# Order of the bank reads in the first pair of a second-matrix pass, and of the last pass's squares

## What is computed

```python
h = rmsnorm(x, norm_ffn[l])
x = x + jnp.square(jax.nn.relu(h @ w_ff1[l])) @ w_ff2[l]      # w_ff1 1024 x 4096, w_ff2 4096 x 1024
return rmsnorm(x, final_norm)                                  # first_block
...
u = rmsnorm_2(x, ln_g[layer])                                  # second_block, layer 0
proj = u @ w_in
```

## Time and profile before

| | |
|---|---|
| median of three runs | 1632.52 us (1631.73 to 1632.7) |
| the profiled execution, its own time | 1632.63 us |
| its span | 1630.9 us, granted clock 0.999 |
| busy share of the span | PE 98%, PEld 83%, DVE 61%, ACT 54%, POOL 48% |
| POOL L830, pieces of 128 x 256 from a raw panel | 864 times, 849 ns in the mean |
| DVE L2557, the adds of the pairs | 112 times, 419 ns in the mean |
| PE L1163 (first of the three products of a turn) | 448 times, 285 ns in the mean |

### The profile page before, as it was taken

One profiled execution on the slowest core, in us unless ns is written; L12 is line 12 of the kernel. 1 busy time (PEld: TensorE's weight loads), 2 busy tenths in 40 slices (PEclk: granted clock), 3 DMA queues, 4 the chain that ended last, 5 costly groups with the idle time before them and its releaser, 6 DMA issues.

```text
span 1630.9 us, 23121 instructions
## 1 busy us (share of the span) xinstructions
PE 1603.0 (98%) x8079; PEld 1349.4 (83%) x8079; DVE 1001.6 (61%) x1563; ACT 874.9 (54%) x1189; POOL 777.2 (48%) x966
## 2 busy tenths in 40 slices
PE   7999999999999999999999999999999999999998
PEld 6888888888888898989897788888888887888886
DVE  3466666631114676758587957447447548688677
ACT  6467777753234544444466645444444446755675
POOL 7453333346656495867679535635635633000000
PEclk9999999999999999999999999999999999999999
DMA  7222221123333233242424222422422423332321
GB/s 210 78 79 63 64 77 58 46 65 116 91 109 98 78 95 112 78 116 79 128 65 118 76 66 78 116 65 78 116 65 66 116 64 93 92 93 68 107 63 62
DMA packets 249053, 143.00 MB, mean 88 GB/s; under 512 B 6161, under 2 KB 245522, under 8 KB 248978
## 3 DMA queue, kind: packets, MB, share of 16 engines
q1 hardware_dynamic: 248978, 142.00, 30.4%
HBM read 139.89 MB, written 2.10 MB: 87 GB/s over the span
## 4 chain that ended last, share of the span: by engine, by line
PE 75%; DVE 2%; issue 1%; POOL 1%; ACT 0%; DVEq 0%
PE bank L897 17%; PE bank L898 17%; PE bank L905 17%; PE bank L1163 3%; PE bank L1168 2%; PE bank L1166 2%; PE bank L888 1%; PE bank L890 1%; PE bank L889 1%; PE bank L1291 1%; PE bank L1272 1%; PE bank L1274 1%; PE bank L1273 1%; PE bank L1417 1%; PE bank L1418 1%
## 5 line engine op out<-in xcount | busy, mean ns | idle before, releaser
L830 POOL TENSOR_TENSOR w_lo<-raw,w_hi 128x256 fp32r<-128x256 f32 x864 | 704.9, 849 | 551.9 <-ACT w_hi L1524 521.3
L897 PE MATMUL bank<-h_hi,w_hi 128*128 128x512 f32 x1252 | 497.1, 397 | 0.0
L898 PE MATMUL bank<-h_lo,w_hi 128*128 128x512 f32 x1252 | 487.9, 390 | 0.0
L1524 ACT ACTIVATE w_hi<-raw 128x1024 fp32r<-128x1024 f32 x232 | 243.5, 1054 | 317.5 <-PE bank L905 263.8
L905 PE MATMUL bank<-h_hi,w_lo 128*128 128x512 f32 x1252 | 309.8, 389 | 0.0
L897 PEld LDWEIGHTS bank<-h_hi,w_hi 128*128 128x128 f32 x1252 | 235.1, 188 | 54.1 <-issue 6.0
L898 PEld LDWEIGHTS bank<-h_lo,w_hi 128*128 128x128 f32 x1252 | 235.1, 188 | 52.0 <-issue 4.1
L905 PEld LDWEIGHTS bank<-h_hi,w_lo 128*128 128x128 f32 x1252 | 235.0, 188 | 49.2 <-issue 0.5
L1163 PE MATMUL bank<-f_hi,w_hi 128*128 128x256 f32 x448 | 127.7, 285 | 6.4 <-DVE xT L2557 5.3
L1166 PE MATMUL bank<-f_lo,w_hi 128*128 128x256 f32 x448 | 126.7, 283 | 0.0
L1168 PE MATMUL bank<-f_hi,w_lo 128*128 128x256 f32 x448 | 126.7, 283 | 0.0
(11 more groups left out here) (465 smaller groups left out, 2852.5 us busy)
## 6 DMA issues: line engine op xcount, KB each, us to landing
raw<-in_w_ff SPq DMA_DIRECT2D x64, 512.0 KB, 4.1
raw<-in_w_in SPq DMA_DIRECT2D x56, 512.0 KB, 3.7
raw<-in_m_w_in SPq DMA_DIRECT2D x48, 512.0 KB, 3.9
raw<-in_r_w_in SPq DMA_DIRECT2D x24, 512.0 KB, 3.9
raw<-in_m_w_out SPq DMA_DIRECT2D x16, 512.0 KB, 3.4
raw<-in_r_w_out SPq DMA_DIRECT2D x16, 384.0 KB, 3.1
raw<-in_w_up_b SPq DMA_DIRECT2D x8, 512.0 KB, 4.1
raw<-in_w_out SPq DMA_DIRECT2D x8, 512.0 KB, 4.1
```

The lines of the kernel that those rows point to most:

```text
L830: return pool.tensor_tensor(w_lo[:, s, part], full, w_hi[:, s, part].bitcast(F32), ALU.subtract)
L897: pe.matmul(dst, w_hi[:, s, c], hi[:, k, :], start=(k == 0), stop=False)
L898: pe.matmul(dst, w_hi[:, s, c], lo[:, k, :], start=False, stop=False)
L1524: act.activation(w_hi[:, p % RING, :], raw[:, p % RING, :], ACT.Copy).then_inc(hi_ready[p % RING], 1)
```

## The change

Two edits.

1. In the first pair of every pass the read of p5 (bank 2) becomes a function `second_read`, written between L2507 and the last lower half of the newest tile (now L2512). The adds behind it run in the order p6, p2, p3, p7, p7, p4 instead of p5, p2, p6, p3, p7, p7, p4, and the weight sum `third` stands behind the second of them as before, `fourth` behind p3 instead of p6. The chain's counts on PE follow: p7 waits for the third read (p6) and p4 for the fourth (p2); p3 still waits for the second (p5).
2. In the last pass ACT squares the tiles 2 and 3 behind the pair c = 2 instead of c = 1, and tile 4 behind the last pair, together with 5 to 7. `add_squares` on DVE is not edited.

```diff
@@ pe, pair @@
                     elif name == "p7":
                         pe.wait_ge(sum_lo_pool, i * (2 * NC) + (2 * c + 1))
-                        read(3 if c else 4)
+                        read(3)
...
                     elif name == "p4":
                         panel_split(pe, p + 1, i, F_N)
-                        read(5 if c else 3)
+                        read(5 if c else 4)
@@ act, ffn @@
-                        for e in [(0, 1), (2, 3), (4,), (5, 6, 7)][c]:
+                        for e in [(0, 1), (), (2, 3), (4, 5, 6, 7)][c]:
                             both_squares(e)
@@ dve, forms @@
                            .then_inc(ft_made, 1)
+                        if c == NC - 1:
+                            second_read()
                         dve.wait_ge(fthi_made, i * (3 * NC) + (3 * c + 3))
@@ dve, ffn @@
+                def second_read():
+                    dve.wait_ge(turn_done, i * (FORMS * NC) + turn_at(0, "p5"))
+                    dve.tensor_tensor(xT[:, 1, HALF:S], xT[:, 1, HALF:S], bank[2][:, 0:HALF], ALU.add)\
+                       .then_inc(chain, 1)
...
                     if c == 0:
-                        reads[0] = 1
-                        add("p5", x2[:, right], r2, ALU.add)
+                        reads[0] = 2
+                        add("p6", x1[:, right], r1, ALU.add)
                         add("p2", x1[:, left], r3, ALU.add, before=1)
                         behind(2)
-                        add("p6", x1[:, right], r1, ALU.add)
+                        add("p3", x1[:, right], r2, ALU.add, taken[2 + c % 2], before=3)
                         behind(3)
-                        add("p3", x1[:, right], r2, ALU.add, taken[2 + c % 2], before=4)
                         add("p7", x2[:, left], r1, ALU.add, drained)
```

## The result

| | before | after |
|---|---|---|
| median of the runs | 1632.12 us (4 runs) | 1643.58 us (1642.99 to 1644.18, 4 runs) |
| ratio | | 1.007, 95% interval 1.0058 to 1.0082 |
| the profiled execution, and its span | 1632.63, 1630.9 us | 1644.18, 1642.5 us |
| granted clock of the profiled execution, mean | 0.999 | 0.994 |

The kernel became 11.5 us slower, five times the 2.3 us forecast and outside the range of 1632.9 to 1637.4 us. The view of waits of PE, after, puts POOL first where before it was DVE, with a larger sum.

What follows compares the result with a forecast made beforehand. PE, 98% busy, was taken as the bound, held in first pairs by DVE's bank reads, with POOL 0.15 us behind. Passes one to three 0.93 plus last pass 1.4 gave +2.3 us: median 1634.9, range 1632.9 to 1637.4.

Steps and rivals of the forecast that it cites:

- the 1.9 us: Second pair's p1: PE would be ready 1.9 us sooner, but POOL leaves only 0.15 us of room.
- the 0.12 us of the third pair's p1 in the first pass: An earlier wait for POOL, forecast to vanish, so the first pass loses 0.33 us instead of 0.45.
- the delay is not made up: Behind the second pair's p1, PE is ready last, after POOL, so the 0.30 us delay stays.
- I take one: First pair: one more DVE sum (L2466) meets POOL's pieces, so the second pair's p1 starts 0.30 us later.
- the step on POOL: First pair: POOL becomes the late engine; each DVE sum meeting it costs 0.45 us, p1 starts at 667.72.
- rival 1: First pairs: DVE reaches L2466 first, two meetings, 0.45 us more in each of four passes: 1636.7 us; chance 0.25.
- the main forecast: One meeting per first pair, POOL's piece starting before L2466, plus late squares: 1634.9 us; chance 0.50.
- PE loses 1.3 us there: Last pair: p6 waits for p1's read, queued on DVE behind the late sum of squares, costing PE 1.3 us.

## Why the prediction was wrong

**Right.** The new read costs nothing and lies in DVE's wait; p3 and p7 lose their waits; POOL becomes the last, so the 1.9 us do not arrive and p1 of the second pair comes later than before; the 0.12 us of the third pair's p1 in the first pass goes; the delay is not made up. DVE's idle before the sum of squares was to be 2.6 us and is 2.54. One row was misread, without effect: at 666.30 both reads of p7 stand, not the second half's with two more behind it. The sign of the move was right, its size not. By the starts of the turns and without the clock, the passes one to three lost 2.45 us where 0.93 was forecast, and the last pass 2.48 where 1.4 was; the clock took 5.95 where nothing was forecast.

**Failed first: "I take one" of the step on POOL.** The prediction counted one more meeting of DVE and POOL, 0.30 us, and gave two as a rival at 0.75 with a quarter of the chance, decided by 0.02 us. It was two: 0.80, 0.81 and 0.78. What decided was not the tie I looked at. Before, L2457 came just behind POOL's second piece and waited it out, 1.27 us; after, it came just behind again (665.45 against 665.44), but took 0.68 us, and the piece waited, 1.29. From there DVE was 0.6 us ahead of the working of the prediction, and both L2466 fell among the pieces. So rival 1 had the number of meetings, and about the time of p1, by luck: it let DVE win at the first L2466, but there DVE came 0.03 us behind a piece (667.87 against 667.84) and was held to 1.26 us, as the main forecast had it. The price of a meeting was right: two more made the six pieces 0.98 us longer, 0.49 each against the 0.45 forecast. Rounded to 0.01 us the two ties look alike; in the nanoseconds of the traces they don't. In the kernel before, in the one with the late squares alone, in the one with their sums moved too and in the one with added idle, DVE starts 16 to 23 ns behind the piece and is held, in all 16 passes. In the changed kernel, in the one with the reads alone, in the one with filler and in the one with the late lower halves, it starts between 7 ns behind and 2 ns ahead, and goes first, in all 16. So the meeting turns over with the new order of the reads each time, not by chance; what moved it by these 20 ns I can't tell.

**Failed second: "PE loses 1.3 us there".** 1.35 with the edit alone, so the step holds for it; 2.03 in the changed kernel, where the sum took 1.81 us, near the worst that the prediction allowed (1.38 + 0.7).

**Failed third, and worth most: no term for the clock.** The text worked out an idle of 2.2 us in each pass in one piece, where before there were two of 1.34 and 0.47, and priced it by its length. It is not the length alone: behind an unbroken 2.6 us the clock went to 1.2 GHz in three passes of four, 1.5 us each time, and once in the last pair. The profile's mean clock of 0.999 for the kernel before tells only that the idle it had was harmless. The Trainium skill (TensorE: Matmul & The Clock Gate, Part 1), which says that recent activity sets the clock, bears on just this and was not weighed. Without the clock the change would have cost 5.5 us, slower still and just out of the range; these 5.5 us are in the main the second meeting and the longer sum, on top of what was forecast.

**Open.** Why the second pass was spared, in the changed kernel and in the one with the reads alone, and the first in the kernel with both upper halves ahead on the old reads; the idle there was as long. As the executions of one kernel seem to differ in the number of slow stretches (the five with filler), the order of the program may not be the whole answer. From which idle on the clock falls was not measured: 1.7 us in one piece was harmless in four passes, 2.0 us in the last pair, with 0.6 to 0.7 a few us ahead of it, was not, nor was 2.6 in most passes. Not tried was a kernel in which DVE and POOL have less to share; the fastest version run here has a median of 1632.96 us, so none beats the kernel before.

## What to carry to other kernels

Before a wait is taken away, work out what stands right behind it: here a second engine was 0.15 us from being the limit, and the reordered queue of a third engine (DVE) made it late by 0.8 to 1.0. Ask of every idle of the matrix engine not only how long it is but whether the change joins short ones into one; then add the price of the low clock as a case of its own. A step that others consume (the squares) is moved only together with its consumer (the sum), or the consumer blocks all that is queued behind it; here that took the wait away, though the total gained nothing.

## What the runs showed of the hardware

- TensorE at a granted clock of 0.50 for 3.4 us at a time, beginning 0.4 to 1.6 us behind the end of an idle of 2.0 to 2.8 us, with full clock in between, in most such places and not in all. Filling the idle in three passes with 20 matmuls whose products nobody uses made the kernel 2.6 us faster (3.0 between the profiled executions).
- A DVE instruction of 128 x 512 with both inputs in SBUF makes a POOL piece of 128 x 256 beside it take 1.19 instead of 0.74 us, and up to 1.29, and is itself stretched from 0.69 to as much as 1.28; one of 128 x 256 went from 0.41 to 0.96 beside pieces of 0.92; DVE adds with one input from a bank stay at 0.41 us. Where the two start together, DVE waited the piece out when it came 16 to 23 ns behind (16 of 16 passes) and went first when it came at most 7 ns behind (16 of 16), with 0.6 us for all that follows on DVE.
